# Head norms of two attention layers: the sum of squares as fp32r parts instead of fp32

## What is computed

```python
def _rmsnorm(x, g):
    xf = x.astype(jnp.float32)
    y = xf * lax.rsqrt(jnp.mean(xf * xf, axis=-1, keepdims=True) + EPS)
    return (y * g.astype(jnp.float32)).astype(x.dtype)
...
    qn = _rmsnorm(qa[..., :A_NOPE], a_g_q[:A_NOPE])
    kn = _rmsnorm(kva[..., :A_NOPE], a_g_k[:A_NOPE])
...
    bq = _partial_rope(_rmsnorm(b_q.reshape(b, s, B_HEADS, 2, B_DK), b_g_q), *rope_b)
    bk = _partial_rope(_rmsnorm(b_k.reshape(b, s, B_HEADS, 2, B_DK), b_g_k), *rope_b)
...
    cq = _rmsnorm(c_q.reshape(b, s, C_HEADS, C_DH), c_g_q)
    ck = _rmsnorm(c_k.reshape(b, s, C_HEADS, C_DH), c_g_k)
```

## Time and profile before

| | us |
|---|---|
| median of three timed runs | 3443.97 |
| lowest and highest of them | 3442.32, 3451.32 |
| the profiled execution | 3449.17 |
| its span from first to last instruction | 3447.5 |
| granted TensorE clock in it | 0.998 of full speed |
| hybrid layers in it | about 1290 to 3447 |

### The profile page before, as it was taken

How to read it: one execution, slowest core, us unless ns; L and a number is a source line. 1 busy time by engine, 2 the same in 40 slices (tenths; PEclk the granted TensorE clock), 3 DMA queues, 4 the chain that set the end, 5 groups by cost and what they waited for, 6 DMA issues and landing times. The chain is left out here.

```text
span 3447.5 us, 73317 instructions
## 1 busy us (share of the span) xinstructions
PE 3397.2 (99%) x27998; PEld 3320.1 (96%) x27998; DVE 2158.8 (63%) x3522; ACT 1705.0 (49%) x2796; POOL 198.6 (6%) x216
## 2 busy tenths in 40 slices
PE   8999999999999999999999999999999999999999
PEld 7889999999999999899999999999899999999999
DVE  7677666656656666667655665565667755566565
ACT  5545644434434455645545454454655554554443
POOL 1000100000000025000000000001000000000000
PEclk9999999999999999999999999999999999999999
DMA  5224555555555544344455445554444355444554
GB/s 185 105 97 141 175 183 183 194 182 183 190 180 185 188 171 167 138 148 157 155 194 183 173 157 184 186 200 165 142 148 157 134 186 198 178 159 180 181 198 168
DMA packets 90612, 584.18 MB, mean 169 GB/s; under 512 B 10480, under 2 KB 11120, under 8 KB 28400
## 3 DMA queue, kind: packets, MB, share of 16 engines
q1 hardware_dynamic: 88992, 577.60, 47.3%
q0 software_dynamic: 1488, 4.72, 0.4%
HBM read 580.19 MB, written 2.10 MB: 169 GB/s over the span
## 5 line engine op out<-in xcount | busy, mean ns | idle before, releaser
L191 PE MATMUL bank<-h,w_hi 128*128 128x256 f32 x5728 | 1633.3, 285 | 18.3 <-DVE w_lo L172 11.2
L172 DVE TENSOR_TENSOR w_lo<-raw,w_hi 128x768 fp32r<-128x768 f32 (+5 forms) x1202 | 1348.4, 1131 | 478.5 <-ACT w_hi L161 473.0
L192 PE MATMUL bank<-h,w_hi 128*128 128x256 f32 x5728 | 1603.2, 280 | 0.0
L193 PE MATMUL bank<-h,w_lo 128*128 128x256 f32 x5728 | 1598.7, 279 | 0.0
L161 ACT ACTIVATE w_hi<-raw 128x768 fp32r<-128x768 f32 (+4 forms) x1190 | 1093.7, 967 | 236.3 <-PE bank L193 209.0
L191 PEld LDWEIGHTS bank<-h,w_hi 128*128 128x128 f32 x5728 | 1078.7, 188 | 33.1 <-DVE w_lo L172 11.3
L192 PEld LDWEIGHTS bank<-h,w_hi 128*128 128x128 f32 x5728 | 1080.0, 189 | 2.4 <-issue 1.0
L193 PEld LDWEIGHTS bank<-h,w_lo 128*128 128x128 f32 x5728 | 1079.3, 188 | 0.0
L191 PE MATMUL bank<-mixed,w_hi 128*128 128x256 f32 x2304 | 647.1, 281 | 0.7 <-DVE w_lo L172 0.7
L192 PE MATMUL bank<-mixed,w_hi 128*128 128x256 f32 x2304 | 643.8, 279 | 0.0
L193 PE MATMUL bank<-mixed,w_lo 128*128 128x256 f32 x2304 | 642.0, 279 | 0.0
(11 more groups left out here) (374 smaller groups left out, 2806.1 us busy)
## 6 DMA issues: line engine op xcount, KB each, us to landing
raw<-in_w SPq DMA_DIRECT2D x485, 1024.0 KB, 4.8
raw<-in_w_br SPq DMA_DIRECT2D x96, 512.0 KB, 4.3
raw<-in_w_uq SPq DMA_DIRECT2D x8, 768.0 KB, 4.4
raw<-in_w_ukv SPq DMA_DIRECT2D x8, 512.0 KB, 3.3
bias_t<-in_bias POOLq DMA_DIRECT2D x16, 192.0 KB, 3.1
x<-in_x SPq DMA_DIRECT2D x4, 512.0 KB, 8.1
raw<-in_w_kr SPq DMA_DIRECT2D x4, 512.0 KB, 3.2
out_x<-x SPq DMA_DIRECT2D x3, 512.0 KB, 7.3
```

The lines of the kernel that those rows point to most:

```text
L172: dve.tensor_tensor(w_lo[:, b % 2, c], raw[:, b, c], w_hi[:, b % 2, c].bitcast(F32), ALU.subtract).then_inc(S["lo_done"], 1)
L191: pe.matmul(o, w_hi[:, b % 2, c], a_hi, start=start and k == t0, stop=False)
L192: pe.matmul(o, w_hi[:, b % 2, c], a_lo, start=False, stop=False)
L193: last = pe.matmul(o, w_lo[:, b % 2, c], a_hi, start=False, stop=stop and k == t0 + nt - 1)
```

## The change

In 40 of the 48 head sums (all of B and C, the odd heads of A) the squares are given to TensorE in two parts. ScalarE writes its squares as fp32r to a new buffer `sq_hi`. GpSimd squares q and k again in full precision from `pre` to `sq` (two instructions of 256 columns) and subtracts `sq_hi` from it to `sq_lo` (one of 512 columns). TensorE sums `sq_hi` and `sq_lo` by two fp32r matmuls of 512 columns into the same bank, with `sums_r`, an fp32r copy of the two constant matrices that GpSimd makes once. The second matmul waits for `sq_lo`. The even heads of A are squared by ScalarE straight from PSUM and keep the fp32 sum.

```diff
+        sq_hi = buf("sq_hi", [2, SEQ], F32R)
+        sq_lo = buf("sq_lo", [2, SEQ], F32R)
+        sums_r = buf("sums_r", 2 * P, F32R)
...
         def _(pool):
+            pool.tensor_copy(sums_r[:, :], shared[:, P:3 * P]).then_inc(S["sums_r"], 1)
...
+                def low_squares(T, part, row, at):
+
+                    pool.wait_ge(S["h_ss"], T)
+                    for k in range(2):
+                        pool.wait_ge(S[f"bank{k}"], at)
+                        src = pre[:, row + 3 * k, :]
+                        pool.tensor_tensor(sq[:, k, :], src, src, ALU.mult).then_inc(S["sq_full"], 1)
+                    pool.wait_ge(S["sq_full"], 2 * part + 2)
+                    pool.wait_ge(S["h_sq"], 2 * T + 2)
+                    pool.tensor_tensor(sq_lo[:, :, :], sq, sq_hi[:, :, :].bitcast(F32), ALU.subtract).then_inc(S["sq_lo"], 1)
+
                 with pool.Fori(0, NH // 2) as i:
                     for e in range(2):
                         T = head_no(l, BR_A, 2 * i + e)
                         gated(T, e, T if e == 0 else T - 1)
+                    low_squares(head_no(l, BR_A, 2 * i + 1), split_no(l, BR_A, i), 1, 2 * (n0 - N_FIRST) + 2 * (L_A + i) + 2)
                 with pool.Fori(0, NH) as i:
+                    low_squares(head_no(l, BR_B, i), split_no(l, BR_B, i), 0, 2 * (n0 + L_B + i - N_FIRST) + 1)
                     gated(head_no(l, BR_B, i), 0, head_no(l, BR_B, i))
                 with pool.Fori(0, NH) as i:
+                    low_squares(head_no(l, BR_C, i), split_no(l, BR_C, i), 0, 2 * (n0 + L_C + i - N_FIRST) + 1)
                     pool.wait_ge(S["max0"], 2 * head_no(l, BR_C, i))
...
-            def squares(T, k, src):
+            def squares(T, k, src, dst):
 
                 act.wait_ge(S["h_ss"], T)
-                act.activation(sq[:, k, :], src, ACT.Square).then_inc(S["h_sq"], 1)
+                act.activation(dst[:, k, :], src, ACT.Square).then_inc(S["h_sq"], 1)
...
-            def norm(T, sums=ones):
+            def norm(T, part=None, at=0):
+
                 pe.wait_ge(S["h_sq"], 2 * T + 2)
                 pe.wait_ge(S["h_ln"], T)
-                pe.matmul(m[0][:, :], sums, sq.rearrange("p k s -> p (k s)"), start=True, stop=True).then_inc(S["h_ss"], 1)
+                if part is None:
+                    pe.matmul(m[0][:, :], ones, sq.rearrange("p k s -> p (k s)"), start=True, stop=True).then_inc(S["h_ss"], 1)
+                    return
+                pe.wait_ge(S["sums_r"], 1)
+                pe.matmul(m[0][:, :], sums_r[:, at:at + P], sq_hi[:, :, :].rearrange("p k s -> p (k s)"), start=True, stop=False)
+                pe.wait_ge(S["sq_lo"], part + 1)
+                pe.matmul(m[0][:, :], sums_r[:, at:at + P], sq_lo[:, :, :].rearrange("p k s -> p (k s)"), start=False,
+                          stop=True).then_inc(S["h_ss"], 1)
```

More of the change, by code:

```diff
@@ L1489, in hybrid_layers @@
         g[k] for k in ("load_unit", "split_hi", "split_lo", "split_lo_part", "unit", "unit_tiles", "of"))
-    x, h, ident, ones, ones64, eps = (g[k] for k in ("x", "h", "ident", "ones", "ones64", "eps"))
+    x, h, ident, ones, ones64, eps, shared = (g[k] for k in ("x", "h", "ident", "ones", "ones64", "eps", "shared"))
     bank, m, sqx, tn, rn, mid = (g[k] for k in ("bank", "m", "sqx", "tn", "rn", "mixed"))
@@ L1557, in v_no, with split_no @@
         def v_no(l, br, i):
+            return l * (2 * NH + NH // 2) + (0, NH // 2, NH // 2 + NH)[br] + i
+        def split_no(l, br, i):
             return l * (2 * NH + NH // 2) + (0, NH // 2, NH // 2 + NH)[br] + i
@@ L1695, in _ @@
             for l in range(NL):
+                n0 = base(l)
                 def latent_add(k, src, count):
@@ L1810, in pair_hooks @@
                         act.wait_ge(S[f"bank{b}"], 2 * (base(l) - N_FIRST) + 2 * (L_A + j) + 2)
-                    squares(T + 1, 0, pre[:, 1, :])
-                    squares(T + 1, 1, pre[:, 4, :])
+                    squares(T + 1, 0, pre[:, 1, :], sq_hi)
+                    squares(T + 1, 1, pre[:, 4, :], sq_hi)
                 elif k == 1:
@@ L1869, in pair_body @@
                         act.activation(osq, m[1][:, 0:SEQ], ACT.Square).then_inc(S["qr_sq"], 1)
-                        squares(T, 0, bank[0][:, 0:SEQ])
+                        squares(T, 0, bank[0][:, 0:SEQ], sq)
                         act.activation(pre[:, 0:2, :], bank[0][:, :].rearrange("p (k s) -> p k s", k=2), ACT.Copy).then_inc(S["bank0"], 1)
                     else:
-                        squares(T, 1, bank[1][:, 0:SEQ])
+                        squares(T, 1, bank[1][:, 0:SEQ], sq)
                         act.wait_ge(S["v_tr"], v_no(l, BR_A, i))
@@ L1885, in head_body @@
                         act.wait_ge(S[f"bank{b}"], 2 * (n - N_FIRST) + 1)
-                        squares(T, b, pre[:, 3 * b, :])
+                        squares(T, b, pre[:, 3 * b, :], sq_hi)
                     elif b == 3:
@@ L2369, in pair_hooks @@
                 elif k == 1:
-                    norm(T + 1)
+                    norm(T + 1, split_no(l, BR_A, j))
                     pe.wait_ge(S["bank1"], 2 * (base(l) - N_FIRST) + 2 * (L_A + j) + 2)
@@ L2390, in head_hooks @@
                     pe.wait_ge(S["v_tok"], v_no(l, br, j))
-                    norm(T, ones if br == BR_C else ones64)
+                    norm(T, split_no(l, br, j), 0 if br == BR_C else P)
                 elif k == 1:
```

## The result

| | before | after |
|---|---|---|
| median of four timed runs each, us | 3443.25 | 3488.14 |
| lowest and highest | 3442.32, 3451.32 | 3482.63, 3489.88 |
| ratio, 95% interval | | 1.0121 (1.0108 to 1.0135) |
| profiled execution, us | 3449.17 | 3487.59 |
| its span, us | 3447.5 | 3485.9 |

The kernel became 1.2% slower; forecast were 3485 us, range 3458 to 3505. The total is where the prediction put it, but several of its terms are not, and they partly cancel.

A forecast was written before the change was run, and what follows sets the result against it. TensorE, busy 3397.2 of 3447.5 us, was taken to bound the kernel. Terms 27.6 + 20 + 2.2 - 8.4 = +41 us gave 3485 us against the median 3443.97, 1.2% slower, range 3458 to 3505.

The forecast's parts named there:

- TensorE's own saving: Each changed head sum costs 0.43 instead of 0.85 us, saving 0.42; 40 of them 17 us if no wait came.
- a gain at full price: TensorE sets the time everywhere, so every instruction taken from it counts in full, and every wait is lost in full.
- Branch B: Heads 2 to 7, both layers: sum ends late because sq_lo comes late, +2.3 us each, 12 sums, +27.6.
- the row of 2.83 us: GpSimd's L1691 at 1354.41, 0.93 us when quiet; read as GpSimd waiting for both of two successive VectorE L172 instructions.
- rival 2: GpSimd gets a turn between any two VectorE instructions: B +1.1, A +2.6, pair 0 +0.5, total 3466 us; chance 0.20.
- VectorE's own delay counts as nothing: VectorE's delay, under 1 us in each body, costs nothing because it works a unit ahead.
- Branch A, odd heads: Pairs 1 to 3, six sums: GpSimd's chain starts behind two gate products, score late by +3.3 us each, +20.
- The granted clock stays as it is: Sign expected in the profile after: TensorE's granted clock does not change.
- Pair 0: Branch A, two sums: subtraction ready about 1364.65, score about 1.1 us later each, bounds -0.4 and +1.9; +2.2 together.
- Heads 0 and 1 of B: Four sums whose chain starts a body earlier, so no wait: -0.42 us each.
- C: Branch C, 16 sums: subtraction done half a microsecond before it is needed, no wait, -0.42 us each.
- Rival 3: Branch C slips as well: its 12 later heads wait 0.9 us more instead of saving 0.42, 3501 us; chance 0.17.

The follow-up runs named there:

- the rest part for nothing: Changed kernel with GpSimd's squares and subtraction left out, TensorE summing the fp32r part twice without a wait: 3435.24 us, ratio 0.9973.
- the one with reads alone: Kernel before, plus two GpSimd multiplies and a subtraction on constants per head in B, read by nobody: 3466.54 us, ratio 1.0058.
- squares first: Changed kernel with GpSimd's squares and subtraction placed ahead of the gate products in A and B: 3455.75 us, ratio 1.0032.
- not waited for: Changed kernel with GpSimd's new instructions reading constants, their result unread, and TensorE summing the fp32r part twice without waiting: 3461.91 us, ratio 1.0043.
- the run with the squares back behind the gate product: Changed kernel with A's sums fp32 and, in B, VectorE's division and output rest part ahead of both L172; GpSimd's order unchanged: 3446.65 us, ratio 1.0011.

## Why the prediction came out as it did

- **TensorE's own saving** was 0.42 a sum; measured 0.39 to 0.45 in C, step L2347 to L2349 0.23. That was right. But that 40 of them bring 17 us if no wait comes was wrong: with the rest part for nothing it is 8.6. The step that failed is that every saved microsecond counts in full ("a gain at full price"), which holds only where TensorE's next work is ready. In B heads 2 to 7 the division ends at 1578.58 in the kernel before, 0.2 us before the old sum does, and the next instruction needs it. I had its row (L2065 starts at 1577.83 for 0.75 us) and used it for the turns only.
- **Branch B** was +2.3 a head, measured +1.56: 18.6 us for the 12 instead of 27.6. I took from the row of 2.83 us that both L172 go first. The rows after show strict turns, multiply between the two L172, as rival 2 had it. From them: the second half of the sum starts at 1597.26, 1.16 later than one step (0.23) behind the first, and the transposes at 1598.27, 0.78 later than one step behind the second; less the 0.39 that the sum saves, that is 1.55. So the late rest part by itself would cost 0.8 (rival 2 had 1.1), and the other 0.8 is what neither had: TensorE then waits for the division, whose engine was held up by the same turns. The idle time before the second sum matmul was to be 2.7 us and is 0.99 by the profile. That VectorE's own delay counts as nothing is the sentence that failed in B; the run in which TensorE doesn't wait for GpSimd and the one with reads alone show that this delay by itself is the whole loss there.
- **Branch A, odd heads** was +3.3 each, measured +4.0 (24.1 instead of 20), though the chain took 2.9 us and not 3.9, and TensorE waited 3.4 and not 4.4. That the size is near is luck. In the one pair that kept its clock the loss is 2.49, near the 2.2 that I had for the chain alone. The other five lost 3.7 to 5.0: 1.2 to 2.5 us each are TensorE's halved clock behind the wait. "The granted clock stays as it is" was wrong; it had stood there without a reason. The Trainium skill ("TensorE: Matmul & The Clock Gate", Part 1: The HAM clock gate) has TensorE fall to 1.2 GHz when idle and rise again by work, and the five falls agree; I had the wait of 4.4 us in my own text and didn't put the two together.
- **Pair 0**: +1.1, measured +0.67 and +0.82, but not by the step that was told: the rest part is ready in time, and the score waits for VectorE's scaled heads, as it does where TensorE doesn't wait for GpSimd (+0.63 and +0.91). **Heads 0 and 1 of B**: -0.42, measured -0.2 and -0.43 in the stretches behind them. **C**: right in size and in having no wait; its margin was 2.6 us instead of 0.5, since the multiplies are shorter (0.61 instead of 0.73) and had all but ended when the first L172 began, so that only the subtraction was held up (1.80). Rival 3 is refuted.
- **The sum.** In the layers it was to be +41 and is +36; the medians show +44.9. B was 9 us too dear, A 4 too cheap, and some 9 us of the medians lie outside the layers. That 3485 is met within 3 us is luck in good part: these errors cancel, and the medians differ by the scatter too.
- **The row of 2.83 us** misled because of its operation. It is a TENSOR_SCALAR, and those of the chain are TENSOR_TENSOR. In the kernel before, all four of GpSimd's TENSOR_SCALAR that began within the first of two L172 in immediate succession ended only behind both. The one TENSOR_TENSOR in that place went between them and held up the second, which ends 1.36 us after it:

```profile
1336.09 1.12 POOL L1689 TENSOR_TENSOR x<-x,r 128x256 f32<-128x256 f32 x1
...
1335.67 2.90 DVE L172 TENSOR_TENSOR w_lo<-raw,w_hi 128x768 fp32r<-128x768 f32 x2
```

In the changed kernel the same four stand behind both, and all 12 multiplies of B that begin there go between. The moment of arrival doesn't tell the two apart: the TENSOR_SCALARs begin 0.5 to 0.8 us into the first L172, the multiplies 0.6, two TENSOR_TENSORs of "squares first" 0.9 (1487.52 and 2569.87). Nor does it matter that a TENSOR_SCALAR comes 0.1 us behind its predecessor and the multiplies follow theirs at once: a TENSOR_TENSOR of "not waited for" that came 0.15 behind (1319.80) went between too. So it goes with the operation; why, no run shows. The row that would have corrected the turns lay in the trace of the kernel before.

## What to carry to other kernels

Ask of every saved microsecond what the engine does next: if that is someone else's result, the saving ends there. When work goes to an idle engine, price what it does to its neighbour's instructions, in particular to one on whose result the busy engine waits; here three unread GpSimd instructions a head cost as much in branch B as the changed sums. If the work can go to a moment when the neighbour is ahead, and the neighbour's urgent result before its work for later, the same edit turned from 1.2% slower (all three branches) to 0.4% faster (B and C); in A nothing beyond "squares first" was tried.

## What the runs showed of the hardware

- GpSimd's TENSOR_TENSOR and VectorE's L172 take turns one instruction at a time: 1.44 and 1.90 us instead of 0.96 and 1.49 for VectorE, 1.33 and 1.85 instead of 0.61 for GpSimd. A GpSimd TENSOR_SCALAR that came within the first of two L172 stood behind both (2.83 instead of 0.93).
- VectorE's fp32 TENSOR_SCALAR of one tensor is held up as well: a pair of them took 0.74 instead of 0.55 beside memsets and 1.6 beside a subtraction; even one of 128x2 elements (L2082 after) took 0.37 instead of 0.23. GpSimd isn't held up by it: its multiplies beside the scaling kept 0.62 and 0.61 (1568.60 in the run with the squares back behind the gate product), its subtraction 1.30 (1595.91 after).
- TensorE's granted clock was at half around waits of 3.4 us in five of six cases, and around waits of only 2.0 us in four of six ("squares first"). At waits of 1.6 to 1.8 us ("not waited for") and of 1.0 us (B after) it stayed at 1.00. Waits of equal length did it and didn't. Behind them each microsecond of work at half the clock cost 0.4 to 0.5 us.
- An fp32r matmul of 512 columns has a step of 0.23 us; the two of them replace 0.85 by 0.46. On GpSimd a multiply of 256 columns takes 0.61 to 0.74, a subtraction of 512 columns 1.26 to 1.30 undisturbed.
